# The squares of the next norm are summed by 32 column matmuls instead of a DVE reduction and 4 column matmuls

## What is computed

```python
def rmsnorm(x, w):
    xf = x.astype(jnp.float32)
    y = xf * lax.rsqrt(jnp.mean(xf * xf, axis=-1, keepdims=True) + EPS)
    return (y * w.astype(jnp.float32)).astype(x.dtype)

def trunk(x, p):
    for layer in range(DEPTH):
        h = rmsnorm(x, p['norm_w'][layer, 0])
        m = ssd_mla_mixer(h, ...) if layer % 2 == 0 else gla_mixer(h, ...)
        x = x + rmsnorm(m, p['norm_w'][layer, 1])
        h = rmsnorm(x, p['norm_w'][layer, 2])
        f = conv_ffn(h, ...)
        x = x + rmsnorm(f, p['norm_w'][layer, 3])
```

## Time and profile before

| | |
|---|---|
| median of 3 runs | 1536.59 us (1534.59 to 1538.52) |
| profiled execution | 1535.7 us |
| its span in the profile | 1533.9 us |
| PE busy | 1413.5 us, 92% |
| DVE busy | 768.4 us, 50% |
| ACT busy | 644.5 us, 42% |
| POOL busy | 613.7 us, 40% |
| granted PE clock, mean | 0.965 |

### The profile page before, as it was taken

How to read it: one execution, slowest core, us unless ns; L and a number is a source line. 1 busy time by engine, 2 the same in 40 slices (tenths; PEclk the granted TensorE clock), 3 DMA queues, 4 the chain that set the end, 5 groups by cost and what they waited for, 6 DMA issues and landing times.

```text
span 1533.9 us, 16715 instructions
## 1 busy us (share of the span) xinstructions
PE 1413.5 (92%) x6722; PEld 1154.9 (75%) x6722; DVE 768.4 (50%) x1011; ACT 644.5 (42%) x984; POOL 613.7 (40%) x291
## 2 busy tenths in 40 slices
PE   6699798899999999998799999997999999996997
PEld 6578565777887777776688877886897777775886
DVE  5545497563036677676100754355066767765002
ACT  4453474554243434434323465444434343443221
POOL 2334485113532434344455143413713443444550
PEclk9899999999999999999899999987999999998998
DMA  5123100012222332322232312301222332231331
GB/s 188 55 83 97 35 1 11 25 55 73 94 81 82 97 89 90 96 85 85 60 92 91 122 45 93 85 26 41 83 72 82 95 95 92 88 91 50 91 98 55
DMA packets 36686, 117.76 MB, mean 77 GB/s; under 512 B 3841, under 2 KB 8321, under 8 KB 36609
## 3 DMA queue, kind: packets, MB, share of 16 engines
q1 hardware_dynamic: 35888, 114.63, 24.3%
q10 hardware_dynamic: 720, 2.06, 0.4%
HBM read 114.58 MB, written 2.10 MB: 76 GB/s over the span
## 4 chain that ended last, share of the span: by engine, by line
PE 44%; DVE 26%; ACT 14%; issue 4%; POOL 1%; DVEq 0%; ACTq 0%; POOLq 0%
PE bank L311 12%; PE bank L312 12%; PE bank L313 12%; DVE cbuf L629 11%; ACT cbuf L668 4%; DVE cbuf L633 4%; ACT whi L288 3%; DVE ubuf L638 2%; DVE cbuf L695 2%; ACT g_hi L677 2%; ACT cbuf L674 2%; PE bank L1142 2%; PE bank L1275 1%; PE bank L1276 1%; DVE ebuf L1008 1%
## 5 line engine op out<-in xcount | busy, mean ns | idle before, releaser
L294 POOL TENSOR_TENSOR wlo<-raw,whi 128x1024 fp32r<-128x1024 f32 (+2 forms) x216 | 504.0, 2337 | 808.7 <-ACT whi L288 808.7
L311 PE MATMUL bank<-xw_hi,whi 128*128 128x512 f32 (+1 forms) x1360 | 520.6, 383 | 44.6 <-POOL wlo L294 17.0
L313 PE MATMUL bank<-xw_hi,wlo 128*128 128x512 f32 (+1 forms) x1360 | 507.9, 373 | 0.0
L312 PE MATMUL bank<-xw_lo,whi 128*128 128x512 f32 (+1 forms) x1360 | 507.5, 373 | 0.0
L311 PEld LDWEIGHTS bank<-xw_hi,whi 128*128 128x128 f32 x1360 | 260.7, 192 | 109.5 <-issue 42.1
L288 ACT ACTIVATE whi<-raw 128x1024 fp32r<-128x1024 f32 (+2 forms) x217 | 220.2, 1022 | 228.3 <-DMA raw<-in_fout 108.7
L312 PEld LDWEIGHTS bank<-xw_lo,whi 128*128 128x128 f32 x1360 | 260.7, 192 | 45.7 <-issue 3.4
L313 PEld LDWEIGHTS bank<-xw_hi,wlo 128*128 128x128 f32 x1360 | 260.4, 192 | 46.0
L629 DVE SCALAR_TENSOR_TENSOR cbuf<-ubuf,par,cbuf 128x510 f32<-128x510 f32 x100 | 189.1, 1891 | 128.1 <-ACT cbuf L668 115.6
L529 DVE RECIPROCAL small<-small 128x2 f32<-128x2 f32 (+1 forms) x12 | 2.0, 170 | 365.9 <-ACT small L467 342.4
L311 PE MATMUL bank<-g_hi,whi 128*128 128x512 f32 (+1 forms) x396 | 149.1, 377 | 26.9 <-DVE g_lo L698 19.8
(11 more groups left out here) (253 smaller groups left out, 1480.2 us busy)
## 6 DMA issues: line engine op xcount, KB each, us to landing
raw<-in_fin SPq DMA_DIRECT2D x88, 512.0 KB, 3.6
raw<-in_fout SPq DMA_DIRECT2D x32, 448.0 KB, 3.3
raw<-in_gin SPq DMA_DIRECT2D x25, 512.0 KB, 3.6
raw<-in_hin SPq DMA_DIRECT2D x24, 512.0 KB, 3.6
raw<-in_hout SPq DMA_DIRECT2D x16, 512.0 KB, 3.6
raw<-in_fout SPq DMA_DIRECT2D x16, 512.0 KB, 3.5
raw<-in_gout SPq DMA_DIRECT2D x8, 512.0 KB, 3.7
xres<-in_x SPq DMA_DIRECT2D x8, 256.0 KB, 7.6
```

What stands on the lines that cost most here:

```text
L294: engine.tensor_tensor(wlo[s][:, 0:n], raw[s][:, 0:n], whi[s][:, 0:n].bitcast(F32), ALU.subtract).then_inc(w_lo, 1)
L311: first = nc.tensor.matmul(out_ap, wh, ah, start=start, stop=False)
L312: nc.tensor.matmul(out_ap, wh, al, start=False, stop=False)
L313: return first, nc.tensor.matmul(out_ap, wl, ah, start=False, stop=stop)
```

## The change

The DVE reduction goes. PE sums over chunks and partitions at once: for each 128 tokens eight fp32 column matmuls, one for each chunk of the squares, accumulate in the same column of bank 7; 32 per place instead of 4. They wait for ACT's squares directly. The sums move behind chunk 1 and the spread behind chunk 5 of the same block (block 3 in `hin` and `gin`, block 4 in `fin`).

```diff
         def pe_res_sums(pe, k):
-            pe.wait_ge(sem("res_red"), of("res_red", k) + NREQ)
+            sqx = {-1: zbuf, 0: m_hyb, 1: sqx_ffn, 2: m_gla}[k]
+            pe.wait_ge(sem("res_sq"), of("res_sq", k) + NREQ * PAIRS)
             for b in range(NBLK):
-                last = nc.tensor.matmul(bank[7][:, 4 + b:5 + b], sqacc[:, b * P:(b + 1) * P], ones[:, 0:1],
-                                        start=True, stop=True)
+                for c in range(KD):
+                    last = nc.tensor.matmul(bank[7][:, 4 + b:5 + b], ck(sqx, c)[:, b * P:(b + 1) * P], ones[:, 0:1],
+                                            start=c == 0, stop=c == KD - 1)
             last.then_inc(sem("res_ss"), 1)
@@
-        def dve_res_rstd(dve, k, sqx):
-
-            for r in range(NREQ):
-                dve.wait_ge(sem("res_sq"), of("res_sq", k) + (r + 1) * PAIRS)
-                nc.vector.tensor_reduce(of_request(sqacc, r),
-                                        sqx[:].rearrange("p (c r s) -> p r s c", c=KD, r=NREQ)[:, r], AX.X,
-                                        ALU.add).then_inc(sem("res_red"), 1)
+        def dve_res_rstd(dve, k):
+
             dve_diagonal(dve, slice(12, 16), ubuf[1][:], ("res_sd", of("res_sd", k) + 1),
                          ("res_rs", of("res_rs", k) + 1), "res_dg")
@@ pe_fin
-                        beside={4: lambda: pe_res_sums(pe, k)} if j == g else
-                        {2: lambda: pe_res_spread(pe, k)} if j == g + 1 else None)
+                        beside={1: lambda: pe_res_sums(pe, k), 5: lambda: pe_res_spread(pe, k)} if j == g else None)
@@ pe_hin (pe_gin in the same way, with k = 1)
-                        beside={6: lambda: pe_res_sums(pe, -1)} if j == 3 else
-                        {2: lambda: pe_res_spread(pe, -1)} if j == 4 else None)
+                        beside={1: lambda: pe_res_sums(pe, -1), 5: lambda: pe_res_spread(pe, -1)} if j == 3 else None)
```

More of the change, by code:

```diff
@@ L250, in build_program @@
         PER_HALF |= {"res_t": NREQ * PAIRS, "res_x": NREQ * PAIRS}
-        PER_NORM = {"res_hi": NREQ * KD, "res_lo": NREQ * KD, "res_sq": NREQ * PAIRS, "res_red": NREQ, "res_ss": 1,
+        PER_NORM = {"res_hi": NREQ * KD, "res_lo": NREQ * KD, "res_sq": NREQ * PAIRS, "res_ss": 1,
                     "res_sd": 1, "res_rs": 1, "res_dg": 1, "res_sp": 1, "res_rstd": 1}
@@ L1470, in block @@
                 product(pe, base + j, gbank(j)[:], xw_hi, xw_lo,
-                        beside={6: lambda: pe_res_sums(pe, 1)} if j == 3 else
-                        {2: lambda: pe_res_spread(pe, 1)} if j == 4 else None)
+                        beside={1: lambda: pe_res_sums(pe, 1), 5: lambda: pe_res_spread(pe, 1)} if j == 3 else None)
             def gate(t):
@@ L1995, in _ @@
             dve.wait_ge(sem("ident_in"), 16)
-            dve_res_rstd(dve, -1, zbuf)
+            dve_res_rstd(dve, -1)
             dve_hin(dve)
@@ L2002, in _ @@
             dve_res(dve, 0, m_hyb)
-            dve_res_rstd(dve, 0, m_hyb)
+            dve_res_rstd(dve, 0)
             dve_fin(dve, 0)
             dve_res(dve, 1, m_ffn)
-            dve_res_rstd(dve, 1, sqx_ffn)
+            dve_res_rstd(dve, 1)
             dve_gin(dve)
@@ L2009, in _ @@
             dve_res(dve, 2, m_gla)
-            dve_res_rstd(dve, 2, m_gla)
+            dve_res_rstd(dve, 2)
             dve_fin(dve, 1)
```

## The result

The changed kernel takes 1573.96 us (1573.54 to 1574.62), before 1535.59 us: ratio 1.0249, 95% interval 1.023 to 1.0268. That is 38.4 us slower, where 32.7 were forecast. The profiled execution took 1574.6 us, its span is 1572.8 us.

What follows compares the result with a forecast made beforehand. DVE work behind rstd was taken to bound hin, fin0 and fin1, PE to bound gin. With 14.6 us at full clock and 4.5 us of clock loss per place, 3 x 7.3 + 10.8 = 32.7 us gave 1568.4 us, range 1549 to 1577.

Steps and rivals of the forecast that it cites:

- Removal at 0: At all four places: removing DVE's reductions, about 31 us in all, gains 0 because none is on the path.
- Pace of the columns: Column matmuls at four places: 0.1115 us a record at full clock, 0.213 us at half clock, set by weight loads.
- The rival with columns not bound by their loads: Columns at all four places: records step well below 0.1 us, giving 1528.8 us; chance 0.03.
- No new wait, the spread on time: Around sums and spread: ACT's squares and the rstd steps are ready before PE needs them, so no new wait arises.
- At full clock 14.6 us: All four stages, clock not falling: 2.8 us each in hin, fin0, fin1 and 6.24 in gin, giving 1550.3 us.
- the rival in which the clock holds: All four column stretches: the clock does not fall, giving 1550.3 us; chance 0.14.
- PE's extra work is covered in `fin` and counts whole in `gin`: PE's extra 6.24 us a place: hidden by the block 6 wait in fin0 and fin1, wholly on the path in gin.
- The rival in which all of PE counts: All four places: PE's 10.8 us each count in full, 43 us, giving 1579 us; chance 0.06.
- The clock falls in all four stretches: Column stretches at all four places: granted clock falls to 0.50, costing 4.5 us each (2.9 to 7.0).
- the two terms for when it falls and when it comes back: Each column stretch: clock falls after 3.8 us, costing 3.0 us; returns after 3.2 us of wide work, costing 1.5 us.
- PE's wait at the end of `fin0` unchanged: End of fin0: PE's wait of 10.8 us for the last g_lo stays the same.
- the likeliest case: Whole kernel: the clock falls as forecast, 1568.4 us with its own range of 1562 to 1578; chance 0.73.

Runs made afterwards that it cites:

- e5: The changed kernel with DVE's two reductions put back at each place, their result read by nobody: 1573.69 us, ratio 1.0241 to the kernel before.
- after: The changed kernel itself, as measured and profiled with the whole change in place: 1573.96 us, ratio 1.0249 to the kernel before.
- e3: The changed kernel, each column matmul given 120 equal columns of ones instead of 1, ACT reading one of them: 1552.28 us, ratio 1.0114 to the kernel before.
- e7: The kernel before with 28 unread fp32 matmuls of 120 columns added behind the spread in block 5 of fin0 and fin1: 1533.73 us, ratio 0.9986.
- e8: The kernel before with 28 unread fp32 matmuls of 120 columns added in gin, block 4, ahead of the gate matmul: 1543.83 us, ratio 1.0048.
- e1: The kernel before, reductions and 4 column matmuls kept, sums and spread moved behind chunks 1 and 5 of one block at all four places: 1528.31 us.
- e4: The changed kernel, column matmuls in four groups behind chunks 1, 3, 5, 7, spread behind chunk 2 of the next block: 1561.31 us, ratio 1.0165.

## Why the prediction was right in kind and short in size

- *Removal at 0.* Right: e5 differs by 0.3 us, with 31 us of DVE put back.
- *Pace of the columns.* Right at both clocks: 0.1115 and 0.2135 us for a record in after, 0.1115 and 0.213 taken. One column or 120 make no difference to it (e3). The rival with columns not bound by their loads is out. By the Trainium skill, page "TensorE: Matmul & The Clock Gate", section "LDWEIGHTS (loading the stationary operand)", which has a load cost its columns / 1.2, 107 ns, with no word of the clock, the slow records would have kept the fast pace. The trace of after has them at 0.2135 us and those ahead of the fall at 0.1115, so here the figure fits at 2.4 GHz only.
- *No new wait, the spread on time.* Right: no wait stands in front of the columns or the spread in `fin0` of after, where the spread comes at 501.98, 16.4 us after the first column at 485.6. (It was to stand 14 to 16 us behind the start of its block, which is 1 chunk earlier, 484.94; that is 17.0, the size missed below.)
- *At full clock 14.6 us.* Right by stage: the openings of e3 are 2.8, 2.8, 6.2 and 2.8 us longer, 14.6 in all. Its total is 16.7 us above before, interval 14.9 to 20.1, so the sum lies just outside; in the profiled execution 1.1 us of it were there before the block of `hin` began. That is also the rival in which the clock holds, made true: the sum for it was sound, its condition did not come about.
- *PE's extra work is covered in `fin` and counts whole in `gin`.* Right: e7 and e8. In after the wait in front of block 6 is 0.48 us, and from the first scaling on `fin0` loses nothing (19.3 us at its start, 19.4 at its end). The rival in which all of PE counts is out, although its 43 us lie near the 38.4 measured: a total alone would have spoken for it, the steps by stage speak against it.
- *The clock falls in all four stretches.* Right. The sizes taken for it were the error: the two terms for when it falls and when it comes back. It fell 2.8 us after the first column (mean of 3.2, 2.6, 1.9, 3.4), not 3.8, so 38.5 records were slow, not 30: 38.5 x 0.102 = 3.9 us in place of 3.0. It came back 4.5 us after the last column (mean of 6.1, 4.9, 3.7, 3.1), not 3.2: 4.5 x 0.46 = 2.1 in place of 1.5. That is 6.0 us a place where 4.5 stood, and 32.7 + 4 x 1.5 = 38.7 us, against 38.9 in the spans. The clock's own price, measured by e3, is 21.7 us by the medians, or 5.4 a place, and 6.1 by the openings; 4.5 was the term. Both values had been taken from the middle of three rows that didn't agree, and what came lies between the ends (2.9 and 7.0). No row bore on transposes, which the prediction set beside narrow work: in the kernel before none of the 136 records of its transposes started while the clock was at 0.50.
- *PE's wait at the end of `fin0` unchanged.* Wrong: 7.99 us, and 10.76 in the earlier trace rows. Its end moved with the DVE chain as foretold (19.4 us), and so did the start of PE's work on the `g` parts ahead of it (715.37 before, 734.76 after, 19.4 us). But that work ran at a clock of 0.50 at first: 6.04 us x 0.46 = 2.8 us longer, which is what the wait lost. At the end of `fin1` it went the other way, 9.09 us before and 10.62 after: there the kernel before had 3.4 us at 0.50 (1386.2 to 1389.6), some 1.6 us, and after had none. A stretch of after, in `fin0`:

```profile
734.76:740.80 6.04, 6.04 (x14) 4.78 (x15) 3.54 (x4) 2.97 (x4) 3.13 (x2) 0.50 0.00 0
```

- *Range and chances.* The time lies in the likeliest case and 5.6 us above its point.

The openings of the stages, each against before:

| | forecast at full clock | e3, full clock | forecast | measured, after |
|---|---|---|---|---|
| `hin` | 2.8 | 2.8 | 7.3 | 9.3 |
| `fin0` | 2.8 | 2.8 | 7.3 | 9.3 |
| `gin` | 6.2 | 6.2 | 10.8 | 12.8 |
| `fin1` | 2.8 | 2.8 | 7.3 | 7.7 |
| sum | 14.6 | 14.6 | 32.7 | 39.0 |

Between the stages 0.8 us were added from `hin` to `fin0`, 0.4 up to the block of `gin`, and 1.0 came back between `gin` and `fin1`.

## What to carry to other kernels

Before work is moved from an idle engine to one that is on the path in some stage, ask stage by stage which of the two is late there: 31 us of DVE time were worth nothing here, 25 us of PE time ahead of rstd cost 24 (e3 against e1), and 12.5 us of it behind rstd in `fin` cost nothing (e7). A run of 64 records with one moving column and a weight load each was busy in the profile, and still the clock fell; where such a run can't be avoided, give it wide rows of the same constant (120 columns cost the same here and saved 21.7 us) or set it in small groups between wide matmuls. And look at where a result is asked for before changing how it is made: moving the old sums and spread alone, in three of the four stages, gave 9.7 us.

## What the runs showed of the hardware

- PE busy without a gap didn't hold the clock. With one-column matmuls it fell to 0.50 after 1.9 to 3.4 us and came back only 3.1 to 6.1 us into wide work (after). With 120 columns at the same pace it stayed at 1.00 through 7.2 us, four times of four (e3).
- In the same one-column work, in groups of 16 records with 1.4 us of wide matmuls between, it stayed at 1.00 in three places of four (e4); in `gin` it was at 0.50 for 3.4 us.
- fp32 matmuls with their own weights step 0.1115 us a record with 1 moving column (after) and with 120 (e3) at 2.4 GHz, and 0.2135 us with one column at 1.2 GHz.
- In `gin` of e1 PE waited for 0.45 and 1.59 us within 3.5 us, and 6.8 us at 0.50 followed, which by the loss of 46% cost some 3.1 us more. It is one case, so that the pauses brought the fall isn't shown.
- The same PE work doesn't always lose the clock at the same point: in `hin` it fell 3.2 us after the first column in after and 4.2 us in e5.
